# Ten weight pieces of a portion's first blocks are loaded into buffers that stand empty, and those blocks are moved ahead of the first gathered rows

## The reference

```python
for l in range(DEPTH):                       # DEPTH = 2
    xp, _, cp = _mixing_sublayer(xp, kp, vp, zero_past, lw)
    xp = xp + _peer(_rmsnorm(xp, ffn_g[l]), wq[l], keys[l], u[l], v[l])
    xs, vns, cs = _mixing_sublayer(xs, cache_k[l], cache_v[l], state_conv[l], lw)
    xs = xs + _peer(...)
# mixing: h = rmsnorm(x) @ w_in, then a gated MLP, a gated 31-tap convolution
# (glu = val_b * sigmoid(gate_b)), cross-attention into 256 memory rows, and
# x + merged @ w_out, merged = the sum of three gated branches
# peer, for each token and each of 8 heads:
#   v1, i1 = top_k(s[:, :, 0], 16); v2, i2 = top_k(s[:, :, 1], 16); the 16 best pairs -> eid
#   hid = gelu(einsum('bd,bhkd->bhk', xb, u_tab[eid]))
#   y   = einsum('bhk,bhkd->bd', g * hid, v_tab[eid])
```

## Time and profile before

| | us |
|---|---|
| median of 3 runs (lowest, highest) | 2416.97 (2414.62, 2418.0) |
| profiled execution, its own time | 2417.97 |
| its span in the trace | 2416.1 |
| TensorE matmul busy | 1646.6 (68%) |
| VectorE busy | 1605.6 (66%) |
| GpSimd busy | 694.7 (29%) |
| ScalarE busy | 688.4 (28%) |
| moved by the 16 DMA engines | 906 MB, 375 GB/s in the mean |

### The profile page before, as it was taken

The page is one execution under the profiler, slowest core; times in us unless marked ns, Lnnn a source line. Parts: engine busy times, 40 slices in busy tenths (PEclk is TensorE's granted clock), DMA queues, the critical chain, the costliest instruction groups (busy, mean ns, idle before and its releaser), DMA issues.

```text
span 2416.1 us, 32671 instructions
## 1 busy us (share of the span) xinstructions
PE 1646.6 (68%) x11464; PEld 1149.0 (48%) x11464; DVE 1605.6 (66%) x4267; ACT 688.4 (28%) x1699; POOL 694.7 (29%) x608
## 2 busy tenths in 40 slices
PE   8989848457898638966888536746899853343333
PEld 7889827235786306744666304623678610000000
DVE  3282156887756677779765566788675767777774
ACT  2122143331142325232232224323113232333221
POOL 0000032223223333323333243222322344444442
PEclk9999969778899759977889756867889865555555
DMA  7566799799899999999999999979979999999996
GB/s 269 205 240 219 260 362 418 284 409 381 356 390 421 420 421 411 420 422 399 382 419 420 421 421 413 400 274 406 390 306 413 420 408 422 421 422 421 421 414 280
DMA packets 127842, 905.98 MB, mean 375 GB/s; under 512 B 16112, under 2 KB 16576, under 8 KB 18368
## 3 DMA queue, kind: packets, MB, share of 16 engines
q0 software_dynamic: 82944, 604.02, 60.7%
q1 hardware_dynamic: 44736, 299.90, 31.2%
HBM read 895.75 MB, written 8.11 MB: 374 GB/s over the span
## 4 chain that ended last, share of the span: by engine, by line
PE 40%; DMA 24%; DVE 22%; ACT 4%; issue 4%; DVEq 4%; POOL 2%; POOLq 0%; ACTq 0%
PE bank L1089 23%; DMA uv<-uv_in,idx_u 20%; DVE uv L997 8%; PE bank L1095 6%; PE bank L1397 5%; DVE yB L689 4%; DMA ring<-cache_in 2%; POOL uv L360 2%; DMA ring<-w_in 1%; DVEq L684 1%; DVE tmp_s L699 1%; DVE yB L704 1%; ACT L423 1%; ACT diag L634 1%; DVE x L1018 1%
## 5 line engine op out<-in xcount | busy, mean ns | idle before, releaser
L360 POOL DMA_INDIRECT uv<-uv_in,idx_u x576 | 652.7, 1133 | 1526.0 <-PE bank L1397 1156.9
L997 DVE CUSTOM_DVE_ANT_0 uv<-uv,xrep 128x1024 f32<-128x1024 f32 x576 | 681.5, 1221 | 221.4 <-DMA uv<-uv_in,idx_u 221.0
L1397 PE MATMUL bank<-uv,diag 128*32 128x512 f32 x2304 | 443.1, 853 | 522.9 <-ACT diag L634 522.6
L1089 PEld LDWEIGHTS bank<-xnT,ring 128*128 128x128 f32 x4096 | 545.1, 200 | 99.6 <-issue 91.8
L1089 PE MATMUL bank<-xnT,ring 128*128 128x128 f32 (+1 forms) x4096 | 570.0, 299 | 17.9 <-ACT yMA L423 15.3
L1397 PEld LDWEIGHTS bank<-uv,diag 128*32 128x32 f32 x2304 | 55.4, 126 | 774.3 <-ACT diag L634 716.1
L423 ACT ACTIVATE pick<-pick 128x2 f32<-128x2 f32 (+1 forms) x324 | 69.5, 215 | 1110.5 <-DVE pick L997 1109.9
L689 DVE SCALAR_TENSOR_TENSOR yB<-ext_p,small,yB 128x128 f32<-128x128 f32 x960 | 286.7, 360 | 20.3 <-issue 1.3
L423 ACT ACT_TABLE_LOAD x169 | 216.8, 1283 | 11.4 <-DMA x<-x_in 4.6
L634 ACT ACTIVATE diag<-gated_fold,pick 128x32 f32<-128x32 f32 x576 | 153.6, 314 | 9.8 <-DVE gated_fold L1007 0.3
L1089 PE MATMUL bank<-yMA,ring 128*128 128x128 f32 (+1 forms) x1024 | 140.6, 291 | 7.5 <-DVE merged L869 7.5
(11 more groups left out here) (158 smaller groups left out, 1583.7 us busy)
## 6 DMA issues: line engine op xcount, KB each, us to landing
ring<-w_in SPq DMA_DIRECT2D x224, 1024.0 KB, 10.3
ring<-cache_in SPq DMA_DIRECT2D x32, 1024.0 KB, 14.9
uv<-uv_in,idx_u POOLq DMA_INDIRECT x576, 15.5
phase<-rows_in SPq DMA_DIRECT2D x4, 1024.0 KB, 7.4
ring<-keys_in SPq DMA_DIRECT2D x4, 1024.0 KB, 9.2
ext_s<-state_in SPq DMA_DIRECT2D x2, 1088.0 KB, 11.1
convs_out<-ext_s SPq DMA_DIRECT2D x2, 1088.0 KB, 26.6
ext_s<-mem_in SPq DMA_DIRECT2D x2, 1024.0 KB, 14.7
```

The lines of the kernel that those rows point to most:

```text
L360: nc.gpsimd.indirect_dma_start(out=uvbuf[2 * b + i], out_offset=None, in_=uv_in, in_offset=bass.IndirectOffsetOnAxis(ap=ids[:, c:c + 1], a ...
L997: ins = V.tensor_tensor_reduce(out=u, in0=u, in1=xrep[gg % 2][:, :], scale=1.0, scalar=0.0, op0=ALU.mult, op1=ALU.add, accum_out=hid[:, c: ...
L1089: ins = MM(out, w[:, k, P * b:P * (b + 1)], rhs(k), start=k == 0, stop=k == KB - 1)
L1397: ins = MM(vbank[gg % 2][c:c + 32, :], diag[:, t % 4, i], uvbuf[2 * b + i][:, D + 512 * n:D + 512 * (n + 1)], start=first, stop=last)
```

## The change

Before the first gathers, all ten `uvbuf` buffers are empty. The change puts the first ten pieces of portion 1 (`glu0` to `glu7`, `q0`, `q1`) there. They are taken out of the ring's list, and SyncE issues them during portion 0's merges: one behind each of the loads of `mg0` to `mg9`. The buffers must then be emptied before the first rows can come: `gather(0)` to `gather(4)` now wait for TensorE to have used `glu1`, `glu3`, `glu5`, `glu7` and `q1`. So the first blocks of portion 1 are brought forward: its rows are turned and `glu0` to `glu3` done before slot 0 on TensorE, `glu4` and `glu5` after slot 0, `glu6` and `glu7` after slot 1, `q0` and `q1` after slot 2. The rest of portion 1 is spread from slot 2 on.

Two smaller edits go with it, in both odd portions: the turning of the sample tokens' probabilities (`pts`) stands between `va1` and `va2` instead of behind `va3`, and the places given to `va` and `out` pieces shrink from 6.9 to 4.8. On SyncE's queue the reload of the memory keys and values of portion 1 now stands ahead of `q3`, and its convolution stores stand behind `ck1`.

```diff
+EARLY = items(1)[:2 * SLOTS]
+ITEMS = [it for m in range(PORTIONS) for it in items(m) if it not in EARLY]
...
-    out += [(f"va{i}", (3.5, 6.9)[p]) for i in range(4)]
     if p:
-        out += [("pts", 3)] + [(f"sv{n}", 2.5) for n in range(8)] + [("ot", 3)]
+        out += [("va0", 4.8), ("va1", 4.8), ("pts", 3), ("va2", 4.8), ("va3", 4.8)]
+        out += [(f"sv{n}", 2.5) for n in range(8)] + [("ot", 3)]
...
+EARLY_SLOT = 2
 def reach(m, u):
     last = PAIRS * STEPS[(m - 1) % 2] - TAIL
+    if m == 1 and u <= EARLY_SLOT:
+        return PLACE[1][("glu2", "glu4", "glu6", "q0", "q2")[u + 2]] - 0.1
+    if m == 1 and u < last:
+        first = PLACE[1]["q2"]
+        return first + (PLACE[1]["end"] - first) * (u - EARLY_SLOT) / (last - EARLY_SLOT)
     return PLACE[m % 2]["end"] * (u - LEAD) / (last - LEAD) if u < last else 1e9
...
-                    if p == 1 and n == 4:
+                    if n == (0, 11, 0, 4)[m] and p == 1:
                         sp.wait_ge(S["pe_xt"], at("pe_xt", m, 3))
...
-                    load(*it)
+                    if it not in EARLY:
+                        load(*it)
+                    if m == 0 and kind == "mg" and i < len(EARLY):
+                        early = EARLY[i]
+                        r = WROW[early[1:]]
+                        sp.dma_start(uvbuf[i], w_in[P * r:P * (r + 1), :]).then_inc(early_landed[i], 16)
...
                 if t >= SLOTS:
                     pool.wait_ge(S["v_used"], t - SLOTS + 1)
+                else:
+                    name, c = freed(*EARLY[2 * t + 1])
+                    pool.wait_ge(S[name], c)
...
+                if m == 0:
+                    mix(reach(1, -2))
```

More of the change, by code:

```diff
@@ L58, in items @@
     return [(m, k[0], i) for k in kinds for i in range(*k[1:])]
-ITEMS = [it for m in range(PORTIONS) for it in items(m)]
+EARLY = items(1)[:2 * SLOTS]
+ITEMS = [it for m in range(PORTIONS) for it in items(m) if it not in EARLY]
 ITEM = {it: n for n, it in enumerate(ITEMS)}
@@ L113, in parts @@
         out += [(f"sk{n}", 2.5) for n in range(8)]
-    out += [(f"va{i}", (3.5, 6.9)[p]) for i in range(4)]
     if p:
-        out += [("pts", 3)] + [(f"sv{n}", 2.5) for n in range(8)] + [("ot", 3)]
+        out += [("va0", 4.8), ("va1", 4.8), ("pts", 3), ("va2", 4.8), ("va3", 4.8)]
+        out += [(f"sv{n}", 2.5) for n in range(8)] + [("ot", 3)]
+    else:
+        out += [(f"va{i}", 3.5) for i in range(4)]
     out += [(f"mg{i}", h) for i in range(8)] + [(f"ua{i}", h) for i in range(4)] + [(f"sg{i}", 2.5) for i in range(4)]
     out += [(f"mg{i}", h) for i in (8, 9)] + [("csum", 4)] + [(f"mg{i}", h) for i in (10, 11, 12)] + [("csq", 5)]
-    out += [(f"mg{i}", h) for i in range(13, 24)] + [(f"out{i}", (3.5, 6.9)[p]) for i in range(4)]
+    out += [(f"mg{i}", h) for i in range(13, 24)] + [(f"out{i}", (3.5, 4.8)[p]) for i in range(4)]
     out += [("tr2", 12)] + [(f"wq{i}", h) for i in range(4)] + [(f"sc{k}", 1) for k in range(STEPS[p])]
@@ L162, in build @@
         uv_landed = [sem(f"uv_landed{i}") for i in range(SLOTS)]
+        early_landed = [sem(f"early_landed{i}") for i in range(len(EARLY))]
         x_landed = [sem(f"x_landed{t}") for t in range(TILES)]
@@ L260, in landed @@
         def landed(m, kind, i):
+            if (m, kind, i) in EARLY:
+                return early_landed[EARLY.index((m, kind, i))], 16
             n = ITEM[m, kind, i]
@@ L264, in buf @@
         def buf(m, kind, i):
+            if (m, kind, i) in EARLY:
+                return uvbuf[EARLY.index((m, kind, i))]
             return ring[ITEM[m, kind, i] % RING]
@@ L314, in _ @@
                         sp.dma_start(phase[:, 2 * D:4 * D], memv_out[rows_l, :]).then_inc(kv_landed, 16)
-                    load(*it)
+                    if it not in EARLY:
+                        load(*it)
                     kind, i = it[1:]
-                    if p == 1 and (kind, i) == ("q", 3):
+                    if m == 0 and kind == "mg" and i < len(EARLY):
+                        early = EARLY[i]
+                        r = WROW[early[1:]]
+                        sp.dma_start(uvbuf[i], w_in[P * r:P * (r + 1), :]).then_inc(early_landed[i], 16)
+                    if p == 1 and (kind, i) == (None, ("ck", 1), None, ("q", 3))[m]:
                         sp.wait_ge(S["glu"], at("glu", m, 8))
@@ L408, in _ @@
             stepper(mixing(0))(1e9)
+            early = stepper(mixing(1))
+            early(reach(1, -1))
             for t in range(SLOTS):
@@ L411, in _ @@
             for m in range(PORTIONS):
-                mix = stepper(mixing(m + 1)) if m + 1 < PORTIONS else None
+                mix = early if m == 0 else stepper(mixing(m + 1)) if m + 1 < PORTIONS else None
                 for u in range(PAIRS * STEPS[m % 2]):
@@ L531, in mixing @@
                         ins.then_inc(S["va"], 1)
+                    if p and i == 1:
+                        yield place["pts"]
+                        act.wait_ge(S["pe_pts"], at("pe_pts", m, 1))
+                        act.wait_ge(S["pe_o"], at("pe_o", m, 3))
+                        A(probT[0], B[0][:, 0:M], ACT.Copy, "pt_s")
                 act.wait_ge(S["lnv"], at("lnv", m, 1))
@@ L537, in mixing @@
                 if p:
-                    yield place["pts"]
-                    act.wait_ge(S["pe_pts"], at("pe_pts", m, 1))
-                    act.wait_ge(S["pe_o"], at("pe_o", m, 3))
-                    A(probT[0], B[0][:, 0:M], ACT.Copy, "pt_s")
                     yield place["sv7"]
@@ L1256, in mixing @@
                         across_sample(B[4 + i % 2], lambda k: xnT[:, k, P:nt], w).then_inc(S["pe_va"], 1)
-                if p:
-                    yield place["pts"]
-                    pe.wait_ge(S["p_s"], at("p_s", m, 1))
-                    pe.wait_ge(S["pt"], at("pt", m, 4))
-                    for i in range(2):
-                        ins = nc.tensor.transpose(B[0][:, P * i:P * (i + 1)], prob[0][:, P * i:P * (i + 1)], ident)
-                    ins.then_inc(S["pe_pts"], 1)
+                    if p and i == 1:
+                        yield place["pts"]
+                        pe.wait_ge(S["p_s"], at("p_s", m, 1))
+                        pe.wait_ge(S["pt"], at("pt", m, 4))
+                        for j in range(2):
+                            ins = nc.tensor.transpose(B[0][:, P * j:P * (j + 1)], prob[0][:, P * j:P * (j + 1)], ident)
+                        ins.then_inc(S["pe_pts"], 1)
+                if p:
                     for n in range(NSEQ):
@@ L1404, in _ @@
                 mix = stepper(mixing(m + 1)) if m + 1 < PORTIONS else None
+                if m == 0:
+                    mix(reach(1, -1))
                 for u in range(PAIRS * STEPS[m % 2]):
```

## The result

| | median | runs | ratio to before |
|---|---|---|---|
| before | 2417.31 us | 4 (2414.62 to 2418.0) | |
| after | 2434.82 us | 4 (2434.66 to 2438.75) | 1.0078, 95% interval 1.0061 to 1.0096 |

The change makes the kernel slower by 17.5 us, where the forecast said 9 (2426); the measured 2434.82 lies 0.8 above the forecast's own range (2418 to 2434). The profiled execution of after took 2434.96 us, its span is 2433.0 against 2416.1.

What follows compares the result with a forecast made beforehand. From 318 us on, time was taken as bytes over 421 GB/s plus time in which the DMA engines aren't full; 8 - 17.5 + 33 - 12 - 2 = +9.5 us gave a 2426 median, own range 2418 to 2434, wider range 2404 to 2440.

Steps and rivals of the forecast that it cites:

- rivals that ended at 2417 and 2404: Wash, 2417, chance 0.22: later stages regain the start's cost. Faster, 2404, chance 0.20: bytes win, later holes nearly vanish.
- slow rival: Much slower, 2438, chance 0.13: slots 3 to 9 become VectorE's, later holes don't shrink, the start costs 34 us.
- Part 1: Prologue, portion 0's merges: ten early loads crowd the queue and TensorE gets `ua0` late; +8 us, range 3 to 11.
- Part 2: Portion 0's slots: seven pieces fewer (11 in place against 4) to move while DMA engines are full; -17.5 us.
- Part 3: Start of portion 0's slots: first five gathers wait for TensorE's blocks, DMA engines lack 14.0 MB; +33 us, bounds 22 to 40.
- Part 4: Later holes in portion 0's slots shrink from 32.7 us of DMA emptiness to 21; -12 us, bounds 0 to -25.
- The attention's hole: Around 440 to 480, VectorE and TensorE waiting for each other: 13 of 16.8 us of emptiness stay.
- GpSimd's: The hole at 590 in portion 0's slots, read as GpSimd's own work: its 4.0 us stay.
- the `sg` steps: Hole at 650 to 670, a gather's wait with three `sg` steps between slots; now at most two, 4 of 10.4 us left.
- Part 5: Portion 2's slots, portion 3's mixing: `pts` and places move, one hole goes; -2 us, range +3 to -5.

Runs made afterwards that it cites:

- e_places: Kernel before with only the two small edits (`pts` behind `va1`, smaller places), no early pieces, blocks not ahead: 2409.74 us, 0.9963 of the kernel before.
- the spread version: Changed kernel with its ten early pieces issued behind every second merge piece, `mg4` to `mg22`, instead of `mg0` to `mg9`: 2428.36 us, 1.0040 of the kernel before.
- the waits alone: Changed kernel's order without early pieces, gathers 0 to 4 still waiting for `glu1`, `glu3`, `glu5`, `glu7`, `q1`: 2433.70 us, 1.0061 of the kernel before.

## Why the prediction was right in sign and short in size

The forecast's mechanism is the one that ran: the first gathers wait, the DMA engines stand empty for 34 us more, and the bytes moved ahead pay back half. The rivals that ended at 2417 and 2404 are out. The slow rival's 2438 is nearer to the measured time than the forecast's 2426, and its price for the start, 34, is what was measured; but its path did not run, since the later holes shrank by 8.9 where it had 0, and from 416 to 446, where it had VectorE as the limit, the DMA engines are at 1.01. In steps of ratio, each from a pair of runs: small edits -8.9 us, blocks ahead -7.5, waits +31.2, ten pieces -5.1, their place in the prologue +9.2; together the change's own 1.0078. Each difference is uncertain by some 4 us; of the pairs only the one on the ten pieces has intervals that touch; in that pair and in the one on the waits the two versions ran on different chips, each beside the kernel before.

- **Part 1, +8 forecast.** The first indices were 10.05 us late. `ua0` was at 189.93 (187.5 forecast). The 64 `va` matmuls, begun at 137.52 in both and ahead of the first early load (143.01), took 15.46 us and not 14.05, at a granted clock of 0.58 from 137 to 141 where before had 1.00. If all of that 1.4 came through, the queue's own part is 8.5; that is not shown, since in e_places, with no early load, they took 15.52 and the indices still came at 318.16, 0.3 later than before. The ring waits that the step forecast are there, 5.95 us in four, and the spread version has none. The step held. One reading in it is loose: the earlier trace rows's 275 ns is the length of one pipelined matmul record, while 128 of them in 14.46 us stand 113 ns apart; the sum uses the 14.46.
- **Part 2, -17.5.** In bytes it held: 7.0 MB fewer (forecast 7.3), 16.9 us. But as a gain of its own it is small: ten pieces, spread, bring 5 us against the waits alone, since their bytes leave a stretch that the waits had emptied. Parts 2 and 3 could only be added because part 3 counted the lack of bytes against before.
- **Part 3, +33.** Empty time in the first stretch rose by 34.3. The way there was too short: pairs at 20.7, 29.3, 46.1, 56.0 and 78.2 us after the indices, where the working has 18.6, 27.6, 42.4, 53.1 and 70.6. The last was mis-sized most: dots(3) came 11.0 us after its gather and not 9.2 (the convolution stores are issued in that time, at 390.10 and 390.77; whether they are the reason was not tried), and `q1` took 6.94 us at a lowered clock and not 4.5. The step had the lower clock at the first block alone; it was there again behind each wait. Waiting alone, without pieces, measured 31.
- **Part 4, -12.** Measured -8.9; by the windows under 0.9 it is 23.4 where the earlier trace rows add up to 32.7. The attention's hole kept 12.2 (13 forecast), GpSimd's nothing (4 forecast), and what lies from 636 on kept 9.6 (4 forecast); 1.6 at 406 is new. Two terms were mis-sized. GpSimd's was read as its own work that stays: the work stayed and the hole went, so the work was not the reason by itself. And the `sg` steps, thinned to two between two slots as forecast, shortened the wait there from 14.82 to 10.20 but left 7.5 us of emptiness, with 2.1 more at a wait of 17.20 that came up ahead of them.
- **Part 5, -2.** Measured -4.8 in portion 2's slots, inside its range; -2.6 with the small edits alone.
- **What the sum did not have** is some 5 us of portion 0's slots in which the DMA engines were neither empty nor as full as before (410 and 414 GB/s), and -1.7 in portion 1's and the last slots. The waits alone show the same against the order without them: +31.8 in the slots, of which 19.8 and 6.1 are empty time. In the thirteen traces the rate of the non-empty time in portion 0's slots lies between 410 and 416 GB/s; what lowers it was not pursued.

So portion 0's slots, +3.5 by the sum, came to +13.5: +1.3 from part 3, +0.6 from part 2, +3.1 from part 4 and 5 from the part the sum lacked. What the forecast did not see is which waits make the emptiness. It followed one chain of five waits. The runs show that with slot 0 free four waits leave 20 us empty, and that the bytes taken away pay for just that; with slot 0's wait the same eight pieces leave 33 us empty, and 18 us are lost (11 us with two pieces), and the fifth gather's wait for `q1` adds 7 us for 8. Two runs would separate it further and were not made: slot 0's wait without early loads, and the waits of slots 1 to 4 without them.

Four versions beat both kernels by the same amount within their intervals: none, two, four, or eight early pieces in the last slots' buffers, 0.9932, 0.9921, 0.9921 and 0.9933. The order of the blocks with the small edits holds all of that gain, and no early load adds to it. The one without early loads is the simplest: 2401.83 us, 16.6 us faster than the kernel before.

## What to carry to other kernels

A buffer that stands empty is not free if the next stage's first transfer has to wait for it. Count what is lent by the slot. Here, with the first slot's buffers kept free, each gather went out a slot of work ahead of its dots, and the loans from the second slot on came out even; with the first slot's lent too, VectorE stood before the rows for 9 us in slots 0 and 2 and for 3 to 4 in slots 1 and 3. And moving bytes ahead pays only if the stretch they leave stays full; separate the order of a change from its transfers, since here the order alone held all of the gain.
